# Window attention scores of query tiles 1 to 3 computed from rounded, stacked halves of q and doubled k; query rotations one pair earlier

## The reference

```python
def rope(x, positions):
    half = HEAD_DIM // 2
    ...
    x1, x2 = xf[..., :half], xf[..., half:]
    return jnp.concatenate([x1 * cos - x2 * sin, x2 * cos + x1 * sin], axis=-1).astype(x.dtype)

def banded_window_attention(q, k, v, sink):
    ...
    qb = q.reshape(b, nb, BLOCK, N_KV_HEADS, GQA_GROUP, HEAD_DIM)
    ...
    kb, vb = band(k), band(v)
    scores = jnp.einsum("bnqkgd,bnskd->bnkgqs", qb, kb).astype(jnp.float32) * (HEAD_DIM ** -0.5)
    ...
    p = jnp.exp(scores - m[..., None])
    denom = jnp.sum(p, axis=-1) + jnp.exp(sink_f - m)
    o = jnp.einsum("bnkgqs,bnskd->bnqkgd", p.astype(v.dtype), vb).astype(jnp.float32)
    ...

def second_block(x, ...):
    for l in range(DEPTH):
        x = layer_norm(ALPHA * x + 0.5 * swiglu(x, ffn1_w_gu[l], ffn1_w_down[l]), ln1_g[l], ln1_b[l])
        x = layer_norm(ALPHA * x + hybrid_mixer(x, w_in[l], ...), ln2_g[l], ln2_b[l])
        x = layer_norm(ALPHA * x + 0.5 * swiglu(x, ffn2_w_gu[l], ffn2_w_down[l]), ln3_g[l], ln3_b[l])
    return x
```

## Time and profile before

| | before |
|---|---|
| median of 3 runs | 3416.85 us (3416.82 to 3416.97) |
| profiled execution, its own time | 3418.57 us |
| its span in the profile | 3416.8 us |
| PE busy | 3391.7 us (99%) |
| DVE busy | 2505.0 us (73%) |
| ACT busy | 1572.3 us (46%) |
| pair loop, mixer of layer 0 | 2025 to 2108 us of the span |
| pair loop, mixer of layer 1 | 2913 to 2996 us |
| mean granted TensorE clock | 0.998 of full |

### The profile page before, as it was taken

The page is one execution under the profiler, slowest core; times in us unless marked ns, Lnnn a source line. Parts: engine busy times, 40 slices in busy tenths (PEclk is TensorE's granted clock), DMA queues, the critical chain, the costliest instruction groups (busy, mean ns, idle before and its releaser), DMA issues.

```text
span 3416.8 us, 50613 instructions
## 1 busy us (share of the span) xinstructions
PE 3391.7 (99%) x19622; PEld 2906.5 (85%) x19622; DVE 2505.0 (73%) x3075; ACT 1572.3 (46%) x2135; POOL 440.6 (13%) x305
## 2 busy tenths in 40 slices
PE   9999999999999999999999999999999999999998
PEld 6777889988777788998899876899889988679986
DVE  8888568934988657963797388898288937978954
ACT  5555444423455444442444256544254424664433
POOL 3333010001333210001000020200020003120002
PEclk9999999999999999999999999999999999999999
DMA  3111334333221233432443221333333332124332
GB/s 126 62 62 64 110 119 162 103 117 117 69 67 64 76 137 125 132 124 93 145 149 119 96 76 61 120 115 100 123 124 112 99 123 87 61 82 143 100 123 99
DMA packets 98845, 357.23 MB, mean 105 GB/s; under 512 B 10960, under 2 KB 14544, under 8 KB 96976
## 3 DMA queue, kind: packets, MB, share of 16 engines
q1 hardware_dynamic: 85824, 305.68, 27.5%
q10 hardware_dynamic: 12816, 48.70, 3.8%
HBM read 321.83 MB, written 16.78 MB: 99 GB/s over the span
## 4 chain that ended last, share of the span: by engine, by line
PE 90%; DVE 6%; DVEq 2%; ACT 1%; DMA 1%; issue 1%; POOL 0%; SPq 0%; POOLq 0%; ACTq 0%
PE ps L2425 16%; PE ps L2427 15%; PE ps L2426 15%; PE ps L2486 10%; PE ps L2487 10%; PE ps L2485 10%; PE sc L2425 3%; PE sc L2427 3%; PE sc L2426 3%; PE ps L2659 1%; DVE w_lo L1484 1%; PE sc L2731 1%; DVEq L2015 1%; PE sc L2916 1%; ACT w_hi L750 1%
## 5 line engine op out<-in xcount | busy, mean ns | idle before, releaser
L1484 DVE TENSOR_TENSOR w_lo<-raw,w_hi 128x1024 fp32r<-128x1024 f32 x369 | 480.6, 1302 | 468.1 <-ACT w_hi L750 444.0
L750 ACT ACTIVATE w_hi<-raw 128x1024 fp32r<-128x1024 f32 x369 | 390.1, 1058 | 823.2 <-PE sc L2427 404.1
L2425 PE MATMUL ps<-h_hi,w_hi 128*128 128x512 f32 x1352 | 567.6, 420 | 7.5 <-DVE w_lo L1484 3.2
L2427 PE MATMUL ps<-h_hi,w_lo 128*128 128x512 f32 x1352 | 529.2, 391 | 0.0
L2426 PE MATMUL ps<-h_lo,w_hi 128*128 128x512 f32 x1352 | 528.2, 391 | 0.0
L863 ACT ACTIVATE w_hi<-raw 128x1024 fp32r<-128x1024 f32 x204 | 216.4, 1061 | 386.9 <-PE ps L2487 201.3
L2486 PE MATMUL ps<-h_lo,w_hi 128*128 128x256 f32 x1272 | 359.9, 283 | 0.0
L2485 PE MATMUL ps<-h_hi,w_hi 128*128 128x256 f32 x1272 | 359.7, 283 | 0.0
L2487 PE MATMUL ps<-h_hi,w_lo 128*128 128x256 f32 x1272 | 359.7, 283 | 0.0
L2425 PEld LDWEIGHTS ps<-h_hi,w_hi 128*128 128x128 f32 x1352 | 254.8, 188 | 89.5 <-issue 38.9
L2427 PE MATMUL ps<-hid_hi,w_lo 128*128 (+1 forms) x792 | 308.2, 389 | 0.0
(11 more groups left out here) (383 smaller groups left out, 7577.3 us busy)
## 6 DMA issues: line engine op xcount, KB each, us to landing
raw<-wts SPq DMA_DIRECT2D x471, 512.0 KB, 3.4
S<-wts SPq DMA_DIRECT2D x51, 512.0 KB, 3.5
A<-wts SPq DMA_DIRECT2D x51, 512.0 KB, 3.3
x<-parked ACTq DMA_DIRECT2D x7, 2048.0 KB, 8.8
h_hi<-early_hi ACTq DMA_DIRECT2D x15, 512.0 KB, 4.0
h_lo<-early_lo ACTq DMA_DIRECT2D x15, 512.0 KB, 3.5
parked<-x ACTq DMA_DIRECT2D x24, 256.0 KB, 2.0
parked<-x ACTq DMA_DIRECT2D x3, 2048.0 KB, 8.9
```

What stands on the lines that cost most here:

```text
L750: act(w_hi[:, s].rearrange("p a b -> p (a b)"), raw[:, s, :], ACT.Copy).then_inc(s_whi, 1)
L1484: tt(w_lo[:, s].rearrange("p a b -> p (a b)"), raw[:, s, :], w_hi[:, s].rearrange("p a b -> p (a b)").bitcast(F32), ALU.subtract).then_inc ...
L2425: mm(out, w_hi[:, s, b, :], hi, start=start, stop=False, skip_group_check=True)
L2427: return mm(out, w_lo[:, s, b, :], hi, start=False, stop=stop, skip_group_check=True)
```

## The change

For query tiles 1 to 3 the scores are no longer fp32 matmuls over 64 rows, but fp32r matmuls over 128 rows. For each head the stationary operand `q_stacked` holds the rounded part of q in its own 64 rows and the remainder in the other 64. The moving operand is first `k_high_window`, the rounded k of that head in both halves of the rows, and then `k_low_window`, the remainder of k in both halves; both passes add into the same columns. So a pair of these tiles has four passes of 256 or 384 columns. Tile 0 (pairs 0 to 3) is computed as before.

The operands are made once a layer for k and once for each of the three tiles of q, all on 64 rows by 512 columns: ScalarE writes `k_high` in pairs 0 and 1 (two copies each), doubles `k_low` in pair 2 (two copies), and writes the rounded q in pairs 3, 7 and 11 (two copies each); VectorE writes the low part of k in pair 1 and those of q in pairs 3, 7 and 11 (two subtractions each), behind `masked_max`. The rotations of q move from pairs 3, 7 and 11 to 2, 6 and 10; pairs 3, 7 and 11 get two taps in their place (in pair 11 two taps of the short convolution with one tap each, which stood in pair 10). A semaphore that nothing waited for and one of two held ones are gone, which adds and removes no work.

```diff
@@ -345,6 +345,14 @@
         pe2 = [[tmp2(f"window_exps{j}{i}", [P, 3 * P + 1]) for i in range(2)] for j in range(2)]
         pT2 = [[tmp2(f"window_pT{j}{i}", [P, 3 * P]) for i in range(2)] for j in range(2)]
         cc = tmp2("cc_out", [P, 2, SEQ])
+
+        def rounded2(name):
+            tmp2(f"{name}_place", [P, SEQ])
+            return place(name, [P, SEQ], F32R, at=off2[0] - 2 * KB)
+
+        qs2 = [[rounded2(f"q_stacked{j}{i}") for i in range(2)] for j in range(2)]
+        kh2 = [rounded2(f"k_high_window{i}") for i in range(2)]
+        kl2 = [rounded2(f"k_low_window{i}") for i in range(2)]
         high2 = (small[:, 0:2], small[:, 2:4])
         bias2 = (small[:, 4:6], small[:, 6:8])
         sums2 = (small[:, 8:10], small[:, 10:12])
@@ -507,7 +514,10 @@
         q_y = sem("sc_output_ready")
         q_vTp = sem("v2_transposed")
         q_vT = sem("v2_T_ready")
+        own, other = (slice(0, 64), slice(64, P)), (slice(64, P), slice(0, 64))
         q_q = sem("q_rotated_ready")
+        q_sd, q_sh, q_sl = sem("k_low_doubled"), sem("stacked_high_ready"), sem("stacked_low_ready")
+        sd0 = sh0 = sl0 = 0
         q_sc = sem("window_scores_ready")
         q_nm = sem("window_max_ready")
         q_p = sem("window_exp_ready")
@@ -1310,6 +1320,21 @@
                         last = act(held(pe2[j][i], p % QB), held(pe2[j][i], p % QB), ACT.Copy, scale=sums2[j][:, i:i + 1])
                     last.then_inc(q_w, 1)
 
+                def k_high(rows):
+                    eng.wait_ge(q_q, L * 5 + 2)
+                    for i in range(2):
+                        act(kh2[i][rows[i], :], kk2[own[i], :], ACT.Copy).then_inc(q_sh, 1)
+
+                def k_low_doubled():
+                    eng.wait_ge(q_sl, sl0 + 8 * L + 2)
+                    for i in range(2):
+                        act(kl2[i][other[i], :], kl2[i][own[i], :], ACT.Copy).then_inc(q_sd, 1)
+
+                def q_high(t):
+                    eng.wait_ge(q_q, L * 5 + 2 + t)
+                    for i in range(2):
+                        act(qs2[t % 2][i][own[i], :], q2[1][own[i], :], ACT.Copy).then_inc(q_sh, 1)
+
                 def copy_out(p):
                     j = p % 2
                     f0, f1 = frame(p % QB)
@@ -1333,6 +1358,12 @@
                         eng.preload_act_table_set("natural_log_exp_and_others")
 
                 for p in range(PAIRS + 1):
+                    if p < 2:
+                        k_high((own, other)[p])
+                    elif p == 2:
+                        k_low_doubled()
+                    elif p in (3, 7, 11):
+                        q_high(p // 4 + 1)
                     if p < PAIRS:
                         for n in chunks_done_before(p):
                             split_chunk(in0 + n + 2)
@@ -2324,7 +2355,18 @@
                     rotate(kk2, ktmp, T2_K)
 
                 def rotate_q(t):
-                    rotate(q2[t % 2], qtmp, T2_Q + t)
+                    rotate(q2[1 if t else 0], qtmp, T2_Q + t)
+
+                def k_lows():
+                    eng.wait_ge(q_sh, sh0 + 10 * L + 2)
+                    for i in range(2):
+                        tt(kl2[i][own[i], :], kk2[own[i], :], kh2[i][own[i], :].bitcast(F32), ALU.subtract).then_inc(q_sl, 1)
+
+                def q_lows(t):
+                    eng.wait_ge(q_sh, sh0 + 10 * L + 4 + 2 * t)
+                    for i in range(2):
+                        tt(qs2[t % 2][i][other[i], :], q2[1][own[i], :], qs2[t % 2][i][own[i], :].bitcast(F32),
+                           ALU.subtract).then_inc(q_sl, 1)
 
                 def masked_max(p):
                     j, t = p % 2, p // QB
@@ -2367,14 +2409,18 @@
                         masked_max(p)
                     if p in (6, 10, 14):
                         mixed_lo(p // 4 + 1, ps[6 + (p // 4 + 1) % 2][:])
-                    if p in (3, 7, 11):
+                    if p == 1:
+                        k_lows()
+                    elif p in (3, 7, 11):
+                        q_lows(p // 4 + 1)
+                    if p in (2, 6, 10):
                         rotate_q(p // 4 + 1)
                     elif p in (9, 14):
                         short_input(p // 14)
                         convolve(1)
                         short_tap(p // 14, 0)
                         convolve(1)
-                    elif p == 10:
+                    elif p == 11:
                         short_tap(0, 1)
                         convolve(1)
                         short_tap(0, 2)
@@ -2907,14 +2953,23 @@
                 def scores2(p):
                     t, qb = p // QB, p % QB
                     f0, f1 = frame(qb)
-                    eng.wait_ge(q_q, L * 5 + 2 + t)
+                    if t == 0:
+                        eng.wait_ge(q_q, L * 5 + 2)
+                    else:
+                        eng.wait_ge(q_sd, sd0 + 2 * (L + 1))
+                        eng.wait_ge(q_sl, sl0 + 8 * L + 2 + 2 * t)
                     if p:
                         eng.wait_ge(q_nm, P0 + p)
                     k0 = (qb - 1) * P + f0
                     for i in range(2):
                         lo = 64 * i
-                        last = mm(sc[:, i, f0:f1], q2[t % 2][lo:lo + 64, qb * P:(qb + 1) * P],
-                                  kk2[lo:lo + 64, k0:k0 + f1 - f0], start=True, stop=True)
+                        if t == 0:
+                            last = mm(sc[:, i, f0:f1], q2[0][lo:lo + 64, qb * P:(qb + 1) * P],
+                                      kk2[lo:lo + 64, k0:k0 + f1 - f0], start=True, stop=True)
+                        else:
+                            q = qs2[t % 2][i][:, qb * P:(qb + 1) * P]
+                            mm(sc[:, i, f0:f1], q, kh2[i][:, k0:k0 + f1 - f0], start=True, stop=False)
+                            last = mm(sc[:, i, f0:f1], q, kl2[i][:, k0:k0 + f1 - f0], start=False, stop=True)
                     last.then_inc(q_sc, 1)
 
                 def turn2(p):
```

More of the change, by code:

```diff
@@ L401, in build @@
         s_whi = sem("w_hi_ready")
-        s_wlo_pool = sem("w_lo_by_pool_ready")
         s_wlo = sem("w_lo_ready")
@@ L537, in build, with hold @@
         e_copy = sem("token_operands_moved")
-        s_held = [sem("held_dve"), sem("held_pe")]
-        def hold(eng, i, semaphore, value):
+        s_held = sem("held_pe")
+        def hold(eng, semaphore, value):
             eng.wait_ge(semaphore, value)
-            eng.sem_inc(s_held[i], 1)
+            eng.sem_inc(s_held, 1)
         block = ctx.enter_context(nc.Block())
@@ L2566, in down @@
                 turn(0, True)
-                hold(eng, 1, s_hidl, FT * (f + 1))
+                hold(eng, s_hidl, FT * (f + 1))
                 with eng.Fori(1, DOWN_ROWS // 2) as j:
@@ L2767, in _ @@
                     chunk(ps[2 * s][:], s, n=4, b0=0, hi=oa_hi, lo=oa_lo)
-                hold(eng, 1, g_olo, (L + 1) * HEADS)
-                hold(eng, 1, s_bank, L * N_PROJ + N_PROJ + 2)
+                hold(eng, g_olo, (L + 1) * HEADS)
+                hold(eng, s_bank, L * N_PROJ + N_PROJ + 2)
                 for s in range(2):
```

## The result

| | before | after |
|---|---|---|
| median of 16 runs each, side by side | 3417.69 us (3416.61 to 3418.89) | 3424.57 us (3423.72 to 3426.22) |
| ratio, 95% interval | | 1.0021 (1.0014 to 1.0027) |
| span of the profiled execution | 3416.8 us | 3422.7 us |
| layer 0, first to last `masked_max` | 81.94 us | 86.18 us |

The change costs 6.9 us, 0.2%: the forecast's direction and about twice its size (3.6). The two profiled executions differ by 5.9, since that of before lay 0.9 over its median, while that of after lay at its own. The page's line of busy shares, which answers to the earlier trace rows, says little: the span is longer, PE works less, DVE and ACT more.

The account below looks back on a forecast made before the run. PE and DVE were both taken as full in the loops, tied pair by pair. Per layer 3.1 + 2.4 - 3.4 = 2.1 us late, taken as +1.8, +3.6 in all: 3416.85 to 3420.4 us, range 3413 to 3425.5.

Parts of the forecast that it names:

- crumbs: DVE before `masked_max(4)`: 0.4 us of small old idle moments eaten, against 2.4 of subtractions and 1.1 of new waiting.
- I take 0.60: DVE's queue: each new 64-row, 512-column subtraction takes 0.60 us (0.69 without overlap), eight a layer, 4.8 us.
- The wait for the take: Pair 2: DVE's moved rotation waits 1.1 us for ScalarE's take of chunk 7, queued behind the low k's doubling.
- DVE can eat the 3.4 us of waits for scores: Pairs 4 to 15: DVE, late to every group, loses its 3.4 us a layer of waits for score groups.
- Only 3.4 of them are real waits, all for score groups: Of DVE's 5.8 idle us in the loop, 3.4 are real waits, all for scores, in four pairs after pair 4.
- up to 0.7 of DVE's other idle time: Loop's end: up to 0.7 us of other idle time can be eaten, so +1.8 a layer is taken.
- nothing is lost yet: Pair 1: two k subtractions delay `inverses(1)` and `scale(1)`, but the transposes at 2034.87 are just in time.
- some 6 us: Sign in the loop: PE's waits come to some 6 us a layer; otherwise the forecast is wrong.
- PE keeps its gain: Rival: PE bounds the whole, each layer gives 5.1 us, time 3406.6; chance 0.12.
- The passes aren't cheaper: Rival: 256- or 384-column passes cost 0.233 us like 512-column ones, a group 0.93, time 3422.8; chance 0.09.
- VectorE's work adds up in full: Rival: the four waits for scores stay, a layer costs 5.2 us, time 3427.2; chance 0.19.
- The forecast's own upper case: Only half of DVE's 3.4 us of waits for scores goes away, 1.7 more a layer, 3423.9 us.

Follow-up runs that it names:

- e5: The changed kernel with q and k split unstacked: three fp32r passes over 64 rows per head, four 128-row subtractions a layer instead of eight; 3416.96 us.
- e3: The changed kernel with ScalarE's doubling of the low k behind the split and take of chunk 7 instead of ahead of them; 3422.39 us.
- e1: The changed kernel with scores computed as before (fp32 over 64 rows), all new operands still made and waited for, q in two buffers; 3425.91 us.
- e7: The changed kernel with one of the following taps put between the two subtractions of a pair; 3425.22 us (one run).
- e6: The changed kernel with the doubling behind the take of chunk 7 and the two k subtractions a layer made by GpSimd instead of VectorE; 3423.26 us.

## Why the prediction was right, and where it was too small

By its own steps, for one layer. **DVE's balance** from the first to the last `masked_max`: the forecast had 4.8 of work, 1.1 of new waiting, less 0.4 of crumbs and 3.4 of waits for scores, 2.1 late. Measured: 5.3 more busy time and 1.05 less idle time, 4.24 late. The 2.1 us between are three terms (a subtraction's price in the queue, 0.72, is 0.69 of work and 0.03 of idle time behind it):

- **The subtraction's price: 1.0 us.** "I take 0.60" was the wrong end of the pair that the text named (0.60 or 0.69); it is 0.72, above both. Eight times 0.12 is 1.0. The row has 128 rows, and I let it stand for two of 64. e5, with 128 rows, has 0.60.
- **The wait for the take: 0.47 us.** Forecast 1.1, measured 1.57. The mechanism is as told, and e3 shows it. From the end of `scale(1)` the doubling, the split and the take last 2.85 us (2034.65 to 2037.50), not 2.5; and `scale(1)` ends 0.3 later than forecast, behind `inverses(1)` and the dearer subtractions. DVE itself comes 0.2 later.
- **A wait that came back under another name: 0.65 us.** "DVE can eat the 3.4 us of waits for scores" is right by name: none is left. But in pair 6, where DVE had waited 0.92 us for scores, it now waits 0.65 for the rounded mix. ScalarE's queue had been held by DVE's own late maxima of pair 5, and when DVE skips the wait for scores it arrives ahead of that queue. I had asked only which waits vanish, not what is late next. No run takes this wait away by itself; e1 has 0.2 of it. The row of before, beside 2059.23 above:

```profile
2055.74 0.56 DVE L2334 CUSTOM_DVE_ANT_0 window_scores<-sc,band 128x384 f32<-128x384 f32 x1 [0.92 <-PE sc L2916]
```

A smaller reading failed as well. "Only 3.4 of them are real waits, all for score groups" passes over a fifth one, DVE's last split before `masked_max(15)`, which waits 0.70 us for ScalarE's rounding. The forecast let "up to 0.7 of DVE's other idle time" be eaten at the end, and its lower bound (-1.0 a layer) all of it; this wait stands as it was, before and after:

```profile
2107.07 1.23 DVE L1484 TENSOR_TENSOR w_lo<-raw,w_hi 128x1024 fp32r<-128x1024 f32 x1 [0.70 <-ACT w_hi L750]
...
2110.73 1.22 DVE L1515 TENSOR_TENSOR w_lo<-raw,w_hi 128x1024 fp32r<-128x1024 f32 x1 [0.70 <-ACT w_hi L760]
```

**Pair by pair.** Pair 1: "nothing is lost yet" was wrong by 0.41 us, which the transposes waited at 2034.67. Pair 2: the transposes were forecast to lose 1.0 and stood 1.79; pair 3: 0.4 and 0.75. Pair 1 is the first term, passed on, the others the first two. `masked_max(4)`: forecast 3.1 late, measured 4.04. From there to the end: forecast 1.0 won back, measured 0.2 more lost.

**Behind the loop**: the forecast took 0.3 off for the loop's end. Measured is 0.8: a wait of PE for a weight split in the mix's last chunks stood at 2128.37 before and 2131.25 after, which is 2.88 later, where the last `masked_max` was 3.67 later.

```profile
2128.37 0.19 PEld L2425 LDWEIGHTS ps<-mixed,w_hi 128*128 128x128 f32 x1 [0.83 <-DVE w_lo L1484]
2131.25 0.19 PEld L2471 LDWEIGHTS ps<-mixed,w_hi 128*128 128x128 f32 x1 [0.85 <-DVE w_lo L1515]
```

With the 0.57 us by which this execution reached the loop sooner, that is 3.45 us in a layer, 6.9 in two, what the medians differ by.

**PE's side** was right in what a group costs: 0.12 and 0.175 a pass, and in group 5 no idle time ahead. That 6.1 us of new idle time stand where "some 6 us" was forecast is luck. By the forecast 4.1 of gain and 2.1 of delay made 6.2; measured, the delay is 4.24, and PE's busy time in the loop fell by only 1.9 (81.28 to 79.42). About 0.7 of the missing gain is three more passes that fall into the stretch (x468 against x465); the rest isn't worked out. DVE's busy share, forecast above 95%, is 94.5%.

**The rivals.** "PE keeps its gain" is out by e1. "The passes aren't cheaper" is out by the rows. "VectorE's work adds up in full" (5.2 us a layer) is nearer than I had it: 3.45 lies halfway between the forecast's 1.8 and it, since 0.65 of the waits did come back, and the work was 1.0 more. Its own mechanism, that the waits for scores stay, did not happen. The forecast's own upper case (half of these waits stay, 7.0 us in all) didn't either, though it has nearly the measured time: that the time fell inside the range is in part luck, for the price of a subtraction had no term of its own in the range. At 0.21%, interval 0.14 to 0.27%, the result lies on the bound between no change and slower; a single comparison can't tell on which side.

## What to carry to other kernels

Where two engines are tied step by step, a saving on one is worth what the other has free in the same steps: here 8.3 us of TensorE bought 1.3 by the medians, and 11.5 us of new VectorE work cost 9.3. Price each added instruction by a row of the same partitions as well as the same columns, and when a wait is struck off, look for what stands next in the queues that are late too. Before splitting rows to fill an array, ask whether the split doubles the number of instructions that prepare it.

## What the runs showed of the hardware that I had not expected

- A VectorE subtraction over 64 rows by 512 columns isn't cheaper than one over 128 rows, and the one in rows 64 to 127, between instructions that start in row 0, is dearer in the queue: 0.72 us against 0.60, and 0.77 against 0.66 for the tap ahead of it (e7).
- A GpSimd subtraction beside VectorE stretched even an instruction of 128x2 elements from 0.16 to 1.10 us (e6).
- Three fp32r passes over 64 rows for two heads cost 0.91 us at 384 columns with their gaps, because the heads run side by side (the weight loads of a pair are merged into one row of 0.18 us, x2); the two fp32 matmuls cost 1.04 (e5).
